# A decoder block with a mixture of experts: experts fixed for the first 32 blocks, block 0 built by one-hot products, bias rows broadcast by transfers

## The reference

```python
xn2 = rms_norm(h, norm_ffn_g[l]).reshape(B * S, D)
logits = (xn @ w_router + b_router).astype(jnp.float32)
top_val, top_idx = lax.top_k(logits, TOP_K)
gates = jax.nn.softmax(top_val, axis=-1)
...
h = x_pad[toks]
gate = jnp.minimum(h @ w_gate[e] + b_gate[e], SWIGLU_LIMIT)
up = jnp.clip(h @ w_up[e] + b_up[e], -SWIGLU_LIMIT, SWIGLU_LIMIT)
glu = gate * jax.nn.sigmoid(SWIGLU_ALPHA * gate)
return ((up + 1.0) * glu) @ w_down[e] + b_down[e]
```

## Time and profile before

| | us |
|---|---|
| median of the runs before | 1628.29 (1621.68 to 1629.67) |
| the profiled execution | 1625.84 |
| its span, first to last instruction | 1624.1 |
| TensorE busy | 1528.7 |
| VectorE busy | 1298.3 |
| ScalarE busy | 1075.7 |
| GpSimd busy | 405.8 |
| mean granted TensorE clock | 0.968 |

### The profile page before, as it was taken

How to read it: one execution, slowest core, us unless ns; L and a number is a source line. 1 busy time by engine, 2 the same in 40 slices (tenths; PEclk the granted TensorE clock), 3 DMA queues, 4 the chain that set the end, 5 groups by cost and what they waited for, 6 DMA issues and landing times.

```text
span 1624.1 us, 29944 instructions
## 1 busy us (share of the span) xinstructions
PE 1528.7 (94%) x10428; PEld 1263.7 (78%) x10429; DVE 1298.3 (80%) x1442; ACT 1075.7 (66%) x1302; POOL 405.8 (25%) x347
## 2 busy tenths in 40 slices
PE   7999978889859999999999999999999999999982
PEld 6877768877748888888888888888888888888871
DVE  4247555545588999999999999999999999999983
ACT  4245531113337888887888877888878888878871
POOL 7000321101020544422322223222333222223211
PEclk9999999998869999999999999999999999999996
DMA  8311110001548999999999999999999999999973
GB/s 292 95 58 40 40 40 3 4 4 65 207 151 322 401 387 375 388 394 394 388 385 378 390 395 392 385 378 379 379 398 393 379 382 380 398 390 390 380 256 116
DMA packets 78970, 461.63 MB, mean 284 GB/s; under 512 B 10928, under 2 KB 12124, under 8 KB 29756
## 3 DMA queue, kind: packets, MB, share of 16 engines
q1 hardware_dynamic: 69404, 435.56, 67.5%
q0 software_dynamic: 9360, 25.18, 7.2%
q10 hardware_dynamic: 144, 0.00, 0.0%
HBM read 446.02 MB, written 23.59 MB: 289 GB/s over the span
## 4 chain that ended last, share of the span: by engine, by line
PE 89%; DVE 4%; issue 3%; DMA 1%; ACT 1%; POOL 1%; POOLq 0%; DVEq 0%; SPq 0%; ACTq 0%
PE banks L364 75%; PE banks L1662 5%; PE banks L1925 1%; PE banks L1922 1%; PE banks L1755 1%; PE banks L1739 1%; PE banks L1860 1%; PE banks L1907 1%; PE banks L1782 1%; PE banks L1934 0%; DVE expert_w_lo L305 0%; DMA y_sums<-y_block,scatter_rows 0%; PE banks L1971 0%; DMA x_block<-xn_rows,slot_token 0%; DVE residual L1301 0%
## 5 line engine op out<-in xcount | busy, mean ns | idle before, releaser
L305 DVE TENSOR_TENSOR expert_w_lo<-expert_w_raw,expert_w_hi 128x1024 fp32r<-128x1024 f32 x768 | 890.8, 1224 | 72.5 <-ACT expert_w_hi L300 69.3
L300 ACT ACTIVATE expert_w_hi<-expert_w_raw 128x1024 fp32r<-128x1024 f32 x768 | 745.9, 1053 | 5.2 <-PE banks L364 4.0
L364 PE MATMUL banks<-expert_w_hi,x_block_T_hi 128*128 128x512 f32 x992 | 389.6, 393 | 1.1 <-DVE expert_w_lo L305 1.0
L364 PE MATMUL banks<-expert_w_lo,x_block_T_hi 128*128 128x512 f32 x992 | 387.0, 390 | 0.0
L364 PE MATMUL banks<-expert_w_hi,x_block_T_lo 128*128 128x512 f32 x992 | 386.1, 389 | 0.0
L364 PE MATMUL banks<-expert_w_hi,h_block_T_hi 128*128 128x512 f32 x544 | 216.2, 397 | 5.0 <-issue 2.5
L364 PEld LDWEIGHTS banks<-expert_w_hi,x_block_T_hi 128*128 128x128 f32 x992 | 186.4, 188 | 41.3 <-DVE expert_w_lo L305 2.4
L364 PEld LDWEIGHTS banks<-expert_w_lo,x_block_T_hi 128*128 128x128 f32 x992 | 186.2, 188 | 39.6
L364 PEld LDWEIGHTS banks<-expert_w_hi,x_block_T_lo 128*128 128x128 f32 x992 | 186.3, 188 | 37.2
L364 PE MATMUL banks<-expert_w_lo,h_block_T_hi 128*128 128x512 f32 x544 | 213.5, 393 | 0.0
L364 PE MATMUL banks<-expert_w_hi,h_block_T_lo 128*128 128x512 f32 x544 | 213.0, 392 | 0.0
(11 more groups left out here) (362 smaller groups left out, 1938.4 us busy)
## 6 DMA issues: line engine op xcount, KB each, us to landing
expert_w_raw<-in_moe_w_gate_dram SPq DMA_DIRECT2D x128, 1024.0 KB, 8.6
expert_w_raw<-in_moe_w_up_dram SPq DMA_DIRECT2D x128, 1024.0 KB, 5.7
expert_w_raw<-in_moe_w_down_dram SPq DMA_DIRECT2D x128, 1024.0 KB, 8.4
w_raw<-in_w_in_dram SPq DMA_DIRECT2D x24, 512.0 KB, 3.8
residual<-in_x_dram SPq DMA_DIRECT2D x8, 512.0 KB, 4.9
w_raw<-in_w_out_dram SPq DMA_DIRECT2D x8, 512.0 KB, 3.6
y_sums<-v_shifted SPq DMA_DIRECT2D x5, 512.0 KB, 8.8
xn_rows<-xn SPq DMA_DIRECT2D x4, 512.0 KB, 2.7
```

Source lines behind the costliest of these rows:

```text
L300: act.activation(self.hi[:, k % self.nhl, 0:width], self.raw[:, k % self.nraw, 0:width], ACT.Copy)\
L305: dve.tensor_tensor(self.lo[:, k % self.nhl, 0:width], self.raw[:, k % self.nraw, 0:width], self.hi[:, k % self.nhl, 0:width].bitcast(F32) ...
L364: last = pe.matmul(o, lhs, rhs, start=start and t == 0, stop=stop and t == 2, skip_group_check=preset)
```

## The change

- **Experts.** Block i has expert i for i below 32, as a constant; blocks over 31 (none with these inputs) hold the overflow of experts with more than 128 rows. SP no longer reads a table in the main loop, and the tables for the overflow are made in pieces on VectorE during blocks 1 to 6, which are written out (`LOOP0 = 7`).
- **Block 0.** Its x_block is not gathered. `places` makes, for each token tile, a one-hot of the row that a token has in expert 0; `block0_x` multiplies XN2 by it, 32 FP32 products. The contraction is over tokens, so the result is already transposed, with contiguous features; expert 0's gate and up weights are loaded in that order, `first_w`, in rows of 4 KB.
- **Router.** The residual is transposed instead of xn2; norm_ffn_g goes into the router's weights and the row scale into `route`. Transposes, router products and ranks of tiles 0 to 2 stand between the products of the output projection, whose tiles use other bank pairs (`PAIR_OF`).
- **Slots.** A table of 32 columns in 28 products instead of 50 columns in 48; it is built after the fourth gate chunk of block 0.
- **Gates.** The map of gates is stored beside the rows of xn2 in HBM, 32 columns more. A gather brings a row and its gates; GpSimd copies the block's column. The 48 products for the gates go.
- **Biases.** Every bias row is loaded by one transfer that reads it 128 times, into all partitions. `spread_bias` and the 64 partition broadcasts go.

```diff
@@ setup @@
+    PAIR_OF = (2, 3, 0, 1)
+    LOOP0 = 7
...
+    first_w = [t_in[f"moe_w_{n}"][0][0].rearrange("(k p) f -> p k f", p=P) for n in ("gate", "up")]
...
-        def bias_of(name, e):
-            return t_in[name][0][ds(e, 1), :]
+        def bias_rows(name, e):
+            return t_in[name][0][ds(e, 1), :].rearrange("o d -> (o d)").partition_broadcast(P)
@@ SP @@
-            def block_loads(i):
-                e = expert(i)
+            def block_loads(i, e, e_before):
                 sp.wait_ge(S("gate_bias"), i)
-                sp.dma_start(BG[0:1, :], bias_of("moe_b_gate", e)).then_inc(S("gate_bias_in"), 16)
+                sp.dma_start(BG[:, :], bias_rows("moe_b_gate", e)).then_inc(S("gate_bias_in"), 16)
                 loads(i, 0, wg_v, e)
...
             with sp.Fori(0, NE - 2) as it:
-                block_loads(it + 2)
+                block_loads(it + 2, it + 2, it + 1)
@@ GpSimd @@
-            pool.wait_ge(S("xn2_stored"), 16 * TT)
-            pool.wait_ge(S("x2T_ps"), TT)
-            ch.link(pool.memset(XB[:, :], 0.0))
...
+            def keep_gates(i, e, links):
+
+                column = XB[:, D + e:D + e + 1] if isinstance(e, int) else XB[:, ds(e + D, 1)]
...
+            def block_pool(i, e):
+                at = i * 4 - 4 * LOOP0
+                pool.wait_ge(S("xT_ps"), i + 2)
+                keep_gates(i, e, at)
+                gather(i + 1, at + 1)
+                if not (isinstance(i, int) and i == 1):
+                    scatter(i - 2, at + 2, i - 1)
+                    pool.wait_ge(S("y_stored"), i * 16 - 16)
+                y_may_go(i - 1, at + 3)
+
+            pool.wait_ge(S("slots_ok"), 1)
+            pool.wait_ge(S("xn2_stored"), 16 * TT)
+            pool.wait_ge(S("gates_stored"), 16)
+            gather(1, 0)
@@ ACT @@
         def gate_bias(act, i):
-            act.wait_ge(S("bias_spread"), i * 2 + 1)
+            act.wait_ge(S("gate_bias_in"), i * 16 + 16)
@@ VectorE @@
+            def places(tt):
+
+                dve.wait_ge(S("rank_ps"), tt + 1)
+                ch.link(dve.scalar_tensor_tensor(slotm[:, tt, :], MB[:, tt, :], ROW0, bank[2 * PAIR_OF[tt] + 1][:, 0:NE],
+                                                 ALU.mult, ALU.add))
+                dve.tensor_scalar(oh0[:, tt, :], iotaR[:, :], slotm[:, tt, 0:1], None, ALU.is_equal)\
+                    .then_inc(S("rows_ok"), 1)
...
             normed(3)
-            route(2)
-            x2T_dve(3)
-            first_lo(0, 1)
             route(3)
+            first_lo(2, 3)
+            places(3)
@@ TensorE @@
+            def block0_x(tt, a, b):
+
+                pe.wait_ge(S("rows_ok"), tt + 1)
+                pe.wait_ge(S("xn2_ok"), tt + 1)
+                for k in range(a, b):
+                    last = pe.matmul(bank[4 + k // 4][:, (k % 4) * P:(k % 4 + 1) * P], XN2[:, tt, k * P:(k + 1) * P],
+                                     oh0[:, tt, :], start=tt == 0 and k % 4 == 0, stop=tt == TT - 1,
+                                     skip_group_check=True)
...
+            out_units(0, 0, 8)
+            for tt in range(1, TT):
+                out_units(tt, 0, 2)
+                rows_flip(tt - 1)
+                if tt >= 2:
+                    ranks(tt - 2)
+                out_units(tt, 2, 4)
+                logits(tt - 1)
+                out_units(tt, 4, 7)
+                if tt == TT - 1:
+                    ranks(tt - 1)
+                out_units(tt, 7, 8)
```

More of the change, by code:

```diff
@@ new lines, in _ @@
+            pool.wait_ge(S("gates_stored"), 16)
+            gather(1, 0)
+            pool.indirect_dma_start(
+                out=gate0[:, :], out_offset=None, in_=xn2_d,
+                in_offset=bass.IndirectOffsetOnAxis(ap=idx_x[:, 0:1].bitcast(U32), axis=0), element_offset=D,
+                bounds_check=last_x, oob_is_err=False).then_inc(S("gates0_in"), 16)
+            pool.wait_ge(S("gates0_in"), 16)
+            ch.link(pool.tensor_copy(slot_gate[:, 0:1], gate0[:, 0:1]))
+            for i in range(1, LOOP0):
+                block_pool(i, i)
@@ L789, in block_act @@
             hi(0, 5)
-            if not isinstance(i, int):
+            if not (isinstance(i, int) and i == 1):
                 y_act(act, base_of(i), i - 1)
@@ L1124, in lo @@
                     xring.make_lo(dve, base_of(i) + k, UP0 + k)
-            if first:
+            if isinstance(i, int) and i == 1:
                 lo(0, 4)
@@ new lines, in _ @@
+            mixed_add(0, 0)
+            mixed_add(0, 1)
+            mean_square(0)
+            normed(0)
+            mixed_add(1, 0)
+            route(0)
+            mixed_add(1, 1)
+            first_lo(0, 1)
+            mean_square(1)
+            places(0)
+            pair_rows(0)
+            normed(1)
+            route(1)
+            mixed_add(2, 0)
+            mixed_add(2, 1)
+            first_lo(1, 2)
+            mean_square(2)
+            places(1)
+            normed(2)
+            mixed_add(3, 0)
@@ L1614, in _ @@
+            for i in range(1, LOOP0):
+                block_dve(dve, i, over_part)
+            with dve.Fori(0, NE - LOOP0) as it:
+                block_dve(dve, it + LOOP0)
             dve.wait_ge(S("tables_ok"), 1)
@@ L2162, in logits, with ranks @@
                 last.then_inc(S("logits_ps"), 1)
-            out_tile(0)
-            out_tile(1)
-            x2_flip(0)
-            out_tile(2)
-            logits(0)
-            x2_flip(1)
-            out_tile(3)
-            logits(1)
-            x2_flip(2)
-            logits(2)
-            x2_flip(3)
+            def ranks(tt):
+                pe.wait_ge(S("member_ok"), tt + 1)
+                for t2 in range(tt + 1):
+                    last = pe.matmul(bank[2 * PAIR_OF[tt] + 1][:, 0:NE], (triu if t2 == tt else ones_b)[:, :], MB[:, t2, :],
+                                     start=t2 == 0, stop=t2 == tt)
+                last.then_inc(S("rank_ps"), 1)
@@ new lines, in sweep @@
+            def sweep(p):
+                for b in (2 * p, 2 * p + 1):
+                    last = pe.matmul(bank[b], ones_b[:, :], bc(ones_b[:, :], [P, 4, P], 1), start=True, stop=True)
+                last.then_inc(S("banks_swept"), 1)
+            def block0_x(tt, a, b):
[5 more added lines that the diff above has]
+                                     skip_group_check=True)
+                if tt == TT - 1 and b % 4 == 0:
+                    last.then_inc(S("xT_ps"), 1)
@@ L2175, in _ @@
+            rows_flip(3)
+            block0_x(1, 0, 4)
             logits(3)
-            pe.wait_ge(S("member_ok"), TT)
+            block0_x(2, 0, 4)
+            block0_x(0, 4, 8)
+            block0_x(1, 4, 8)
+            ranks(3)
             for tt in range(TT):
-                for t2 in range(tt + 1):
-                    pe.matmul(bank[1][:, tt * NE:(tt + 1) * NE], (triu if t2 == tt else ones_b)[:, :], MB[:, t2, :],
-                              start=t2 == 0, stop=t2 == tt)
-            for tt in range(TT):
-                last = pe.matmul(bank[2][:, 0:NE], ones_b[:, :], MB[:, tt, :], start=tt == 0, stop=tt == TT - 1)
+                last = pe.matmul(bank[6][:, 0:NE], ones_b[:, :], MB[:, tt, :], start=tt == 0, stop=tt == TT - 1)
@@ L2183, in _, with slot_sums @@
             last.then_inc(S("rank_ps"), 1)
-            pe.wait_ge(S("pairs_ok"), 1)
+            block0_x(2, 4, 8)
+            block0_x(3, 0, 4)
+            block0_x(3, 4, 8)
             NP = TT * TOPK
-            for half, parts in ((0, (0, 1)), (1, (2,))):
-                seq = [(v, m) for v in parts for m in range(NP)]
+            def slot_sums(values, n):
+                seq = [(0, m) for m in range(NP)] + [(1, m) for m in range(TOPK, NP)]
                 for z, (v, m) in enumerate(seq):
-                    last = pe.matmul(bank[3][:, half * NBT:(half + 1) * NBT], ohR[:, m, :], rhsv[:, v, m, :],
-                                     start=z == 0, stop=z == len(seq) - 1)
```

528 lines of the change are left out of this document (280 added, 248 removed).

## The result

The changed kernel takes 1641.8 us (median of 4 runs, 1640.5 to 1642.6) beside 1627.2 for the kernel before (4 runs, 1621.7 to 1629.7): a ratio of 1.0105, 95% interval 1.0082 to 1.0129. It is slower by about 1%. The forecast was 1638.

A forecast was written before the change was run, and what follows sets the result against it. TensorE was taken to bound the expert loop, transfers 1.2 us a block short of it, with TensorE mostly idle in the bridge. 1625.8 - 26 (bridge) + 43 (broadcasts) - 5 (given back) = 1638 us, range 1602 to 1660.

The forecast's parts named there:

- The bridge's start: Between output projection and first expert: block 0 starts at 449 instead of 475.2, giving 26 us.
- what follows in block 0 is covered: Block 0: slot table and lower-clock effects offset; gates and block 1's gather, landed near 463, due near 467, cost nothing.
- us for us: Block 0: if the cover fails, TensorE's queue waits behind block 1's gather for as long as it is late.
- The loop: Expert blocks: two bias broadcasts make transfers the bound, 36.0 us a block instead of 34.6, over 30.5 blocks +43.
- 31.6 for bytes and 1.8 for the scatter: Expert block before the change: 13.4 MB at 424 GB/s, plus rate lost beside the scatter, 33.4 us of transfers.
- Given back once: Expert loop: lag builds up before TensorE feels it, and the ring's last round has nothing behind it: -5 us.
- Transfers have room: Rival, expert loop: transfers overlap better, blocks stay at 34.6 to 35.0, time 1600 or 1607; chance 0.20.
- Broadcasts dearer: Rival, expert loop: broadcasts run at 309 GB/s, blocks take 36.8 to 37.0, time 1668; chance 0.13.
- The bridge is longer: Rival, before block 0: low clock and VectorE delay its start to near 461, half the gain gone, 1650; chance 0.10.
- The overflow parts on VectorE and the gates beside the rows: Blocks 1 to 6 and every gather: overflow routing just fits on VectorE, gates add 128 bytes to 4096; both cost nothing.

The follow-up runs named there:

- late transposes: Split-gather, early-spread kernel with block 1's transposes one chunk later on TensorE, its split rows later on ScalarE and VectorE: 1603.3 us, ratio 0.988.
- the kernel with the split: Kernel after with early GpSimd bias spread; block 1's rows gathered before the gates are stored, gates in two small gathers behind: 1609.3 us, ratio 0.989.
- third broadcast: Kernel after plus a third 512 KB bias transfer, read by nobody, in each of blocks 8 to 31 and one ahead: 1680.4 us, ratio 1.035.
- empty rows out: Kernel after, broadcasts kept, with the scatter leaving out the rows of empty slots: 1639.3 us, ratio 1.008.
- odd rows out: Kernel after, broadcasts kept, with scatter rows of odd partitions left out, filled or empty: 1600.9 us, ratio 0.987.
- spread rows: Kernel after, broadcasts kept; empty scatter rows skipped, filled slots placed over the partitions by another pattern, split first gather, later block 1 transposes: 1629.8 us, ratio 1.002.
- one row: Kernel after with each bias transfer from block 2 on bringing one 4 KB row, not 128 copies; nothing spreads it: 1598.6 us, ratio 0.983.
- the kernel before with transfers: Kernel before with only the bias change: both rows brought to all 128 partitions by 512 KB transfers, no GpSimd spread: 1656.5 us, ratio 1.020.
- the spread early: Kernel after with GpSimd spreading biases from block 2, the gate bias spread ahead of its wait for the transposed rows: 1609.4 us, ratio 0.990.

## Why the prediction came out right, step by step

**The bridge's start.** Forecast 449, measured 444.7. The projection's products ended at 433.3 (forecast 435.7; this execution was already 2.0 ahead of the one before some 40 us earlier). The working came to 447.5 and I took 449, so 1.5 of the miss is the margin and 2.4 the projection's end. The price of a one-hot pass lay near my low end of 0.106 and not near twice that: 24 passes in 2.92, some 0.12. The clock stayed up, so the 28 table products took 0.86, not 1.3.

**Block 0.** The step "what follows in block 0 is covered" failed, at the place it named. The gather landed at 465.3, not 463, which would still have met the forecast's 467; but block 0 had started 4.3 early, so TensorE was there at 464.0. The text priced a late gather "us for us"; with 1.3 us of lateness the stretch took 8.6 more than in the kernel before. What it missed is the queue behind: ScalarE and VectorE stood 10 us with weights not yet split, TensorE stood 4.3 for them, and the clock fell after that. The late transposes took back 4, in the kernel with the split. I had forecast -26 for both steps; measured -21.8. That this is close is partly luck: the earlier start hides half of what block 0 gave back.

**The loop.** Forecast 36.0 a block and +43; measured 36.1 and +41.9 over 30 blocks, of which the first 29 cost 44.0 and the last, shorter than in the kernel before, gives 2.1 back. That the broadcasts alone cause it is shown from both sides: without them 34.53, with them in the kernel before 36.0. Their price was 2.5, and the packets bear it out. What was wrong is how the rest of that sum was made, 31.6 for bytes and 1.8 for the scatter, an average over all engines: it misses that leaving out empty rows gains nothing. A sum by the fullest engine, made after the runs, with the median duration of a packet from the records (309 ns for 8 KB of weights, 159 for a bias row, 327 for a scatter row, 167 for a gather row; of a scatter or gather 8 rows are the fullest engine's by the map above), fits each run that the transfers bound within 0.3:

| kernel | weights | bias | scatter | gather | sum | block |
|---|---|---|---|---|---|---|
| after | 96 x 0.309 = 29.7 | 16 x 0.159 = 2.5 | 8 x 0.327 = 2.6 | 8 x 0.167 = 1.3 | 36.1 | 36.1 |
| third broadcast | 29.7 | 3.8 | 2.6 | 1.3 | 37.4 | 37.4 |
| empty rows out | 29.7 | 2.5 | 2.6 | 1.3 | 36.1 | 36.0 |
| odd rows out | 29.7 | 2.5 | 1.3 | 1.3 | 34.8 | 34.8 |
| spread rows | 29.7 | 2.5 | 2.6 | 1.3 | 36.1 | 35.9 |
| one row | 29.7 | 0 | 2.6 | 1.3 | 33.6 | 34.53, TensorE's |

It is a model and not a measurement of one engine: the mean of the weights' packets is longer, 318 ns, and would give some 37. By it the transfers before needed 33.6; that my 33.4 came so close by an average is luck. (The 2.9 that the prediction gives for each further MB is the price of both rows, 1.05 MB.)

**Given back once.** Forecast -5. The last block of the loop took 32.4 in place of 36.1, 3.7, which the +41.9 above already holds. The other half, the first blocks that are not yet held, exists in the kernel before with transfers (two blocks of 34.5) but not here, where block 0's stall had spoiled it. The end is 3.2 shorter, and it is this that fills the place of the -5, for a reason the prediction did not have: without spreads GpSimd's 3.8 us ahead of the last normalisation are gone. That number is luck.

**The rivals.** "Transfers have room" is out: it had blocks of 34.6 to 35.0, and with the broadcasts they take 36.1, and 36.0 in the kernel before. "Broadcasts dearer" is out: it had 36.8, and a third broadcast cost 1.3, not its 1.7. "The bridge is longer" is out at its own place, 444.7 and a clock of 0.96. The overflow parts on VectorE and the gates beside the rows cost nothing while no spread by GpSimd stands behind them, as forecast: the one-row kernel, which has both, runs at TensorE's pace, but for 0.5 us in block 1 and 1.2 us in block 6, where TensorE makes the overflow table.

## What to carry to other kernels

Where the DMA share is 1.00 and TensorE still covers it, count the packets of the fullest engine, not megabytes over a mean rate: a repeated 4 KB row pays in full, and here a scatter whose rows sat in the first half of the partitions cost a block as much as a full one. An operation that costs its own engine nothing may cost a microsecond in each block if something that others wait for stands behind it in the queue; look for the nearest instruction with a waiter before pricing it at zero. A late transfer costs more than its lateness when its consumer's work has been put ahead of independent work in other queues.

## What was not expected of the hardware

- Scatter and gather rows of the first 64 partitions seem to go to 8 of the 16 engines (5 to 9 rows at once for up to 67 rows, against 13 to 17 for 128), and a load spread over all 16 ends with the fullest: half of the scatter's rows left out gave under 0.1 us a block in one place and 1.3 in another.
- GpSimd needs some 4 us more than its waits explain before its first ordinary operation after a spread at the end of the kernel (3.8 and 3.9), as the 7.4 in the earlier trace rows.
- With the spread early, VectorE's product for h_block, which has two operands in SBUF, took 1.76 us in the mean of 23, where the one-row kernel has 1.23. GpSimd's copy of one column took 9.1; in the one-row kernel, which has no spread but the same pace, 5.5; in the kernel before, which has both spreads and that pace, 1.2; in the kernel after, where VectorE has pauses, 0.2:

```profile
L710 POOL COPY scatter_gates<-slot_gate 128x1 f32 x23 | 210.4, 9149 | 227.4 <-DMA y_sums<-y_block,scatter_rows 227.4
...
L1174 DVE SCALAR_TENSOR_TENSOR h_block<-gate_swish,up_act 128x1024 f32<-128x1024 f32 x23 | 40.5, 1759 | 0.8
```

The two engines seem to hold each other up. The Trainium skill's page "SBUF — State Buffer", section "SBUF: two separate sides", says that they share a pair of ports which one of them holds for a whole instruction; these rows do not contradict it, and no run here separates it from other causes.
